# Two transformer blocks on one core: VectorE's queue in the mixing stage is put in another order at two places

## The reference

```python
h = rms_norm(x, mix_norm)
(q_n, kc, vc, ksl, vsl, kwn, vwn, gts, q_s, k_s, v_s) = split(h @ w_in)
# sparse attention: 8 query heads (nq), 2 key heads; three kinds of keys
q   = apply_rope(rms_norm(q_n, g_q), ang)          # four tiles nq 0..3
ks  = apply_rope(rms_norm(ksl, g_ks), ang)         # key tile nk 0
kw  = apply_rope(rms_norm(kwn, g_kw), ang)         # key tile nk 1
kc_ = apply_rope(rms_norm(compress(kc, pe_k, w1_k, w2_k), g_kc), ang_c)   # 31 compressed keys
vc_ = compress(vc, pe_v, w1_v, w2_v)
gates = sigmoid(gts)
def apply_rope(x, ang):   # x1, x2: first two groups of 8 of the 64
    return concat([x1 * cos(ang) - x2 * sin(ang), x2 * cos(ang) + x1 * sin(ang), xp])
```

## Time and profile before

| | us |
|---|---|
| median of 3 runs | 1990.39 |
| lowest and highest of them | 1989.87, 1991.45 |
| the profiled execution, its own time | 1991.26 |
| its span in the profile | 1989.5 |
| PE busy | 1914.2 (96%) |
| DVE, ACT, POOL busy | 779.5, 707.3, 712.6 |
| DMA | 144.22 MB, mean 72 GB/s |
| mean granted clock of TensorE | 0.989 |

### The profile page before, as it was taken

The page is one execution under the profiler, slowest core; times in us unless marked ns, Lnnn a source line. Parts: engine busy times, 40 slices in busy tenths (PEclk is TensorE's granted clock), DMA queues, the critical chain, the costliest instruction groups (busy, mean ns, idle before and its releaser), DMA issues.

```text
span 1989.5 us, 26539 instructions
## 1 busy us (share of the span) xinstructions
PE 1914.2 (96%) x10878; PEld 1631.8 (82%) x10878; DVE 779.5 (39%) x1308; ACT 707.3 (36%) x1328; POOL 712.6 (36%) x343
## 2 busy tenths in 40 slices
PE   7999989999998999999999999899999989999999
PEld 6999878989987887888888877789767768888887
DVE  5433373464326436441112255546666441111001
ACT  3112355321225544232222223446565542222211
POOL 4333201353331114555554423320003325555443
PEclk9999899999999999999999999999999989999999
DMA  4222200122221002323332333210003212222223
GB/s 142 85 82 79 65 1 1 56 83 86 85 85 33 1 22 91 95 92 96 92 95 91 98 102 117 66 42 2 1 0 117 75 54 95 96 95 92 94 88 109
DMA packets 40585, 144.22 MB, mean 72 GB/s; under 512 B 4624, under 2 KB 4880, under 8 KB 40336
## 3 DMA queue, kind: packets, MB, share of 16 engines
q1 hardware_dynamic: 40464, 142.51, 22.2%
HBM read 140.40 MB, written 2.10 MB: 72 GB/s over the span
## 4 chain that ended last, share of the span: by engine, by line
PE 86%; DVE 7%; ACT 3%; DMA 2%; issue 1%; POOL 1%; SPq 0%; DVEq 0%; ACTq 0%
PE ps L354 22%; PE ps L355 22%; PE ps L356 22%; PE ps L849 5%; PE ps L830 5%; PE ps L839 3%; DMA raw<-wstream 2%; PE ps L1994 1%; PE ps L1977 1%; ACT wh L342 1%; PE ps L481 1%; PE ps L966 1%; DVE xl L410 1%; PE ps L1966 1%; POOL wl L350 1%
## 5 line engine op out<-in xcount | busy, mean ns | idle before, releaser
L350 POOL TENSOR_TENSOR wl<-raw,wh 128x1024 fp32r<-128x1024 f32 (+2 forms) x254 | 604.0, 2378 | 855.7 <-ACT wh L342 855.7
L354 PE MATMUL ps<-xh,wh 128*128 128x512 f32 (+1 forms) x1728 | 622.4, 360 | 28.1 <-POOL wl L350 12.9
L355 PE MATMUL ps<-xl,wh 128*128 128x512 f32 (+1 forms) x1728 | 615.6, 356 | 0.0
L342 ACT ACTIVATE wh<-raw 128x1024 fp32r<-128x1024 f32 (+2 forms) x254 | 266.0, 1047 | 978.7 <-PE ps L356 906.5
L356 PE MATMUL ps<-xh,wl 128*128 128x512 f32 (+1 forms) x1728 | 613.6, 355 | 0.0
L354 PEld LDWEIGHTS ps<-xh,wh 128*128 128x128 f32 x1728 | 326.9, 189 | 84.4 <-issue 18.8
L355 PEld LDWEIGHTS ps<-xl,wh 128*128 128x128 f32 x1728 | 327.2, 189 | 50.0 <-issue 1.9
L356 PEld LDWEIGHTS ps<-xh,wl 128*128 128x128 f32 x1728 | 327.7, 190 | 48.3
L1093 POOL TENSOR_TENSOR xl<-xb,xh 128x512 fp32r<-128x512 f32 (+1 forms) x22 | 26.1, 1186 | 328.6 <-ACT xh L1002 328.6
L355 PE MATMUL ps<-aL,wh 128*128 128x512 f32 x352 | 139.3, 396 | 0.0
L356 PE MATMUL ps<-aH,wl 128*128 128x512 f32 x352 | 139.1, 395 | 0.0
(11 more groups left out here) (346 smaller groups left out, 2635.2 us busy)
## 6 DMA issues: line engine op xcount, KB each, us to landing
raw<-wstream SPq DMA_DIRECT2D x236, 512.0 KB, 3.5
raw<-wstream SPq DMA_DIRECT2D x16, 384.0 KB, 3.0
raw<-wstream SPq DMA_DIRECT2D x10, 528.0 KB, 3.6
h<-xT SPq DMA_DIRECT2D x4, 528.0 KB, 6.6
out<-h SPq DMA_DIRECT2D x8, 256.0 KB, 3.9
hm<-memT SPq DMA_DIRECT2D x1, 1024.0 KB, 4.8
cst<-const SPq DMA_DIRECT2D x1, 720.5 KB, 9.6
cst<-const SPq DMA_DIRECT2D x1, 320.0 KB, 4.3
```

Source lines behind the costliest of these rows:

```text
L342: e.activation(wh[p % 2][:, 0:n], raw[c % 2][:, 0:n], ACT.Copy).then_inc(*w_hi(p))
L350: e.tensor_tensor(wl[p % 2][:, 0:n], raw[c % 2][:, 0:n], wh[p % 2][:, 0:n].bitcast(F32), ALU.subtract).then_inc(*w_lo(p))
L354: e.matmul(o, w_h, x_h, start=start, stop=False)
L355: e.matmul(o, w_h, x_l, start=False, stop=False)
```

## The change

Two things are moved, and nothing is added or taken away.

First, the low parts of a rotation become a function of their own (`head_low_dve`). At step 9 the exit of nk 1 is called between the two: after the cosine, sine and add of nq 3, ahead of its low parts.

Second, the third part of the compressed keys moves from step 12 to step 14 on all engines (`KEYS_AT`), that is from behind half 0 of `nv` 1 to behind half 0 of `nv` 2 on PE. On DVE, parts 0 and 1 stay where they were, and part 2 is called at step 14 behind the exits of the first three tiles of `nv` 2.

```diff
+        def head_low_dve(e, on, key):
+            u = scratch[:, 0, 0:head_cols(key)[0]]
             for g, (p0, p1, highs, lows) in enumerate(highs_lows(key)):
...
-        def hooks_dve(e, on, j):
+        def hooks_dve(e, on, j, between=None):
             for what, key in hooks(j):
-                (head_norm_dve if what == "norm" else head_rope_dve)(e, on, key)
-
+                if what == "norm":
+                    head_norm_dve(e, on, key)
+                else:
+                    head_rope_dve(e, on, key)
+                    if between:
+                        between()
+                    head_low_dve(e, on, key)
+
+
+        KEYS_AT = (10, 11, 14)
...
-                    if j < 13:
-                        keys_pe(e, on, j - 10)
+                    if j in KEYS_AT:
+                        keys_pe(e, on, KEYS_AT.index(j))
...
                 if j == 9:
-                    hooks_dve(e, on, j)
-                if key in NORMED:
+                    hooks_dve(e, on, j, lambda: head_out_dve(e, on, key, r))
+                elif key in NORMED:
                     head_out_dve(e, on, key, r)
...
                     hooks_dve(e, on, j)
-                    if j < 13:
-                        keys_dve(e, on, j - 10)
+                    if j in KEYS_AT[:2]:
+                        keys_dve(e, on, KEYS_AT.index(j))
                     if v and half == 0:
                         for i in range(3):
                             values_out(v, i)
+                    if j == KEYS_AT[2]:
+                        keys_dve(e, on, 2)
```

More of the change, by code:

```diff
@@ L1633, in mix_act @@
                     hooks_act(e, on, j)
-                    if j < 13:
-                        keys_act(e, on, j - 10)
+                    if j in KEYS_AT:
+                        keys_act(e, on, KEYS_AT.index(j))
                     if half == 0:
```

## The result

| | before | after |
|---|---|---|
| median, us | 1990.13 (8 runs) | 1983.28 (8 runs) |
| lowest and highest | 1988.36, 1999.30 | 1980.58, 1985.86 |
| the profiled execution: time, span | 1991.26, 1989.5 | 1983.45, 1981.7 |
| mean granted clock | 0.989 | 0.992 |

The ratio is 0.9962, with a 95% interval of 0.9951 to 0.9974: faster by 0.38%. That there is a gain is clear.

What follows compares the result with a forecast made beforehand. PE, busy 96% of the span, was taken to bound the kernel. The sum 4.50 + 1.42 - 0.22 = 5.70 us off the profiled 1991.26 gave 1985.6 us, with an 8-in-10 range of 1984.2 to 1987.2.

Steps and rivals of the forecast that it cites:

- the signs named for being wrong: Low parts later than their high parts allow, tile 2 wait above 1.5 us, gates' wait grown over 0.5, KC or KS wait.
- The exit's place: nk 1's exit right behind nq 3's add, in DVE's gap, costs nothing; PE restarts tile 2 of nv 0 3.30 us sooner.
- The square of nk 1 is late next: Ahead of L1499, a new 0.37 us wait for ACT's square takes some back, leaving 4.50 us net.
- the clock's term: Behind PE's wait for nk 1's exit, 24 matmuls at full clock take 2.95 us instead of 4.52: 1.57 us.
- The second place: Without the compressed keys' rotation, nv 1's exits start 1.42 us sooner; the small matmul moved behind half 0 of nv 2 costs 0.22.
- The last exit and the key tiles: nv 2's last exit is 0.4 us late, which vanishes in the first key exit's 1.11 us of idle time.
- The clock behind the gates: Ahead of tile 1 of nv 2, the 2.12 us wait becomes 1.96, with no fall of the clock expected.
- What it was subtracted from: The 5.70 us came off the profiled execution's 1991.26, taken as 0.87 above the median of the runs.
- more is won: The whole 5.70 us holds for the median, not only the profiled execution: 1984.7; chance 0.12.
- The order of DVE's multiplication and POOL's split: Rival at nk 1: the split starts before L1543, the chain ends 0.7 us later, 1986.3; chance 0.10.
- the clock's rival: At tile 2 of nv 0, timed runs mostly lack low clock, 1986.3, or it stays after the change, 1986.8; chance 0.17.
- The slower case: Merged wait ahead of tile 1 of nv 2 and those behind bring low clock, 1.57 us each, up to 1994.5; chance 0.03.

Runs made afterwards that it cites:

- e2: Only the second part against the kernel before: compressed keys' rotation at step 14, exit of nk 1 left behind the norm of nk 0; 1988.71 us, ratio 0.9985.
- e8: The kernel before, unaltered, compared with itself for a second trace; 1992.12 against 1990.24 us, ratio 1.0013.
- e1: Only the first part against the kernel before: exit of nk 1 between add and low parts, compressed keys still at step 12; 1985.63 us, ratio 0.9975.
- e4: The kernel before with 13 unread matmuls in PE's wait ahead of value tile 2 of nv 0; 1988.88 us, ratio 0.9994.
- e15: The kernel before, unaltered, for a fourth trace of the two waits; a single execution, 1992.40 us.
- e3: The changed kernel again, unaltered, against the kernel before; 1983.88 us, ratio 0.9962.
- e14: The kernel before, unaltered, for a third trace of the two waits; a single execution, 1999.31 us.
- e11: The changed kernel a third time, unaltered, against the kernel before; 1983.95 us, ratio 0.9965.

## Why the prediction was right and wrong

The two mechanisms of the order were right, and none of the signs named for being wrong appeared. Two steps failed: what the sum was taken off, and the clock behind the wait for the gates, a term put at nothing. Some 1.2 us beyond both stay open.

**The exit's place: right.** It starts at the end of the add, in a gap of DVE, and delays neither the low parts nor the norm of nk 0. PE's wait is 0.31 us, where I said 0.6.

**The square of nk 1 is late next: right.** The new wait is 0.23 us, where the sum had 0.37. The first place was to give 4.50 with low clock counted; the first distance went from 20.84 to 16.50, 4.34. Most of the difference is the clock's term: 1.57 in the sum, 1.46 by e2 (20.84 - 19.38), as the matmuls up to L1499 take 3.08 us at full clock and not 2.95.

**The second place, 1.42 less 0.22: right.** The order alone, without low clock on either side, gives 33.97 - 32.69 = 1.28 there. The small matmul at its new place takes 0.14 us to the next start, and that start 0.09 more to the one behind it than is usual: 0.23. That the wait for the gates would be 1.96 and was 2.12 is of the same account: PE came to it earlier than I had worked out, as release and arrival both moved by 1.51 us against the sine of nk 0.

**The last exit and the key tiles: right.** The exit of tile 3 of `nv` 2 is late, and the first key exit has its 1.11 us of slack as before.

**The clock behind the gates: wrong, and this is one of the two steps that failed.** The prediction said of the 2.12 us wait that the clock "did not fall" there, and counted no low clock at the second place on either side. It rested on one trace, and on the sentence that "no wait under 2.2 us here was followed by one". Outside the stage that same trace speaks against it. There PE stood idle for 2.17 and for 1.02 us, and the clock behind was 0.50 and 0.58:

```profile
610.58 0.85 PE L830 MATMUL ps<-KA,QA 128*128 128x144 f32 x2 [2.17 <-ACT Pb L866]
...
726.14 0.76 PE L966 MATMUL ps<-identR,tmpn 128*128 128x128 f32 x4 [1.02 <-DVE tmpn L1068]
```

```profile
610.58:613.00 2.42, 2.42 (x11) 2.42 (x12) 1.61 (x8) 1.51 (x8) 0.06 (x1) 0.50 0.54 154
726.14:728.80 2.66, 2.66 (x9) 2.20 (x10) 0.69 (x1) 0.63 (x1) 0.43 (x1) 0.58 0.01 3
```

As for the wait for the gates itself, in three of four traces of before, and in all three of the changed kernel, low clock does follow it and costs 1.5 us. Against the kernel with both waits filled, the four traces of before hold 21.13 - 19.39 = 1.7 at the first place and 35.13 - 33.97 = 1.2 at the second, 2.9 us in the mean; the sum had 1.57. The traces of the changed kernel keep 1.5 of it, and so the stage's distances give 56.3 - 50.7 = 5.6, close to the forecast, but by luck, as two errors meet: more low clock was there to lose, and not all was lost. The Trainium skill, TensorE: Matmul & The Clock Gate, section What's actually happening, has the phase as free-running; that before shows the same wait for the gates with low clock behind it in three traces, and without in one, agrees. I drew the wrong case from it: the rival took it as less to win, where these runs have more.

**What it was subtracted from: wrong, the other step that failed.** The 5.70 us were taken off the profiled execution's own 1991.26, and that execution was 1.13 above the median of the eight runs, 1990.13. This is half of the 2.3 us between 1985.6 and 1983.28. Its mark ahead of the change, 1244.88, lies 0.9 to 3.0 above that of each of the other sixteen traces, in code that is the same in all. Nothing of this is the change's. The better case, "more is won", with 1984.7, was this; it should have been the forecast's base. The range's lower end, 1984.2, was 5.70 off the lowest of three runs of before, which left next to no room for any other term to be off.

**The rivals.** The order of DVE's multiplication and POOL's split did not flip: the add of nk 1 took 2.25 us and the split 2.82, as before. In all four traces of before low clock follows the first wait, and in none of those of the changed kernel, so by the traces neither way of the clock's rival came. The slower case did not come.

**What stays open.** 5.7 off the median of before, 1990.6, would be 1984.9; measured over all runs it is 1983.8. The distances account for 5.6 of the 6.8 us; the last 1.2 lie outside the stage, for which the sum had nothing, and their cause stays open. Two traces of each kernel without an unusual stretch behind the mark have 689.8 and 689.9 us to the end for before, 689.1 and 689.4 for the changed kernel: 0.6 less, in code that is the same. The whole 1.2 is less than the 1.9 us by which the medians of one kernel differed in e8, so it may be noise. I have no experiment that tells how low clock in a later stage depends on where an earlier one leaves off.

## What to carry to other kernels

A long wait has two causes to look at: who was last, and what the last one did in its queue ahead of it. Here the exit could be put into a gap in which its engine waited for another, and so cost nothing; and a short chain that nobody reads for long, the compressed keys, was standing in front of one that all waited for. When a wait goes, look at once at what stands next to it: the sixth bank alone gave 0.3 us by the order, and 1.4 once the weights' split was moved too. And before a sum is made from one trace, see in a second one whether its clock, and the time ahead of the change, are usual, and look up waits of the same length elsewhere in the first.

## What the runs showed of the hardware

Idle time of PE of 2.1 us was followed by a clock of 0.62 to 0.72 over the next 4.5 to 6 us in seven of the ten traces that have such a wait for the gates, and in three it was not: the first of before, e1 and e4. Idle time of 3.7 us was followed by a clock of 0.50 to 0.66 in five of six, all but e2. Each time it cost 1.3 to 1.6 us beside the wait; once, in e15, 2.6. In the first trace of before idle time of 1.02 us was followed by a clock of 0.58 (above).

Matmuls that nobody reads were put into such a wait six times (twice into the first, four times into the second), and no low clock followed in any of the six; left idle, 12 of 16 waits had it. With both waits filled the kernel before was 3.7 us shorter by the medians and 2.9 by the distances. In the changed kernel they gained 1.5 at their place, which the medians, 0.3 apart, do not show.

Three traces (e3, e8, e14) have a much longer stretch at half clock at the start of the attention. Here is e3's beside the same stretch of e11, the same kernel:

```profile
1314.40:1345.00 30.60, 30.60 (x154) 30.42 (x153) 13.23 (x44) 12.71 (x54) 0.00 (x0) 0.50 0.00 1
```

```profile
1314.40:1345.00 30.60, 28.03 (x244) 26.82 (x243) 19.43 (x64) 18.78 (x76) 1.27 (x1) 1.00 0.01 1
```

PE did 154 matmuls in 30.6 us instead of 244, though it was not idle: busy all of the time at a clock of 0.50. From the first exit of ks to the end e3 takes 700.6 us, e8 700.7 and e14 697.9, and e11 689.4. What sets it off is not shown. The three took 1996.24, 2001.44 and 1999.31 us; the medians do not depend on them.
